# Two residual blocks in one launch: squares summed on GpSimd, compression products on 60 columns, hgrn heads in a loop

## The reference, cut to what matters

```
def rms_norm_2(u, g):                      # the memory's norm (g_mem) and the feed-forward's (g_ffn)
    y = uf * lax.rsqrt(jnp.mean(uf * uf, axis=-1, keepdims=True) + EPS)
    return (y * g).astype(u.dtype)

def compress(u, pe, w1, w2):               # once for keys, once for values; 15 windows of 32 positions, 2 heads
    blk = u[:, tok] + pe[None, None, :, None, :]
    blk = blk.transpose(0, 1, 3, 2, 4).reshape(B, n_cmp, HKV, -1)
    return (jax.nn.silu(blk @ w1) @ w2).transpose(0, 2, 1, 3)

h = rms_norm(x, hgrn_norm[j]); y = hgrn2_mixer(h, ...)   # 16 heads, two directions each
hm = rms_norm_2(mem, g_mem)
hf = rms_norm_2(x, g_ffn); gg, uu = jnp.split(hf @ w_gu, 2, axis=-1)
```

## Time and profile before

| | |
|---|---|
| median of 3 executions | 2378.72 us (2376.79 to 2382.08) |
| profiled execution | 2377.85 us, span 2376.1 us |
| TensorE (PE) busy | 2316.5 us, 97% |
| VectorE (DVE) busy | 1661.3 us, 70% |
| ScalarE (ACT) busy | 1274.4 us, 54% |
| GpSimd (POOL) busy | 226.7 us, 10%, all in the first 330 us |
| mean traffic to and from HBM | 172 GB/s |
| mean granted clock of TensorE | 0.994 |

### The profile page before, as it was taken

How to read it: one execution, slowest core, us unless ns; L and a number is a source line. 1 busy time by engine, 2 the same in 40 slices (tenths; PEclk the granted TensorE clock), 3 DMA queues, 4 the chain that set the end, 5 groups by cost and what they waited for, 6 DMA issues and landing times.

```text
span 2376.1 us, 37247 instructions
## 1 busy us (share of the span) xinstructions
PE 2316.5 (97%) x14226; PEld 2053.9 (86%) x14226; DVE 1661.3 (70%) x2540; ACT 1274.4 (54%) x1438; POOL 226.7 (10%) x53
## 2 busy tenths in 40 slices
PE   6999999999999999999999998989999999999999
PEld 6999988888888888888888877869888888888888
DVE  6777776778878887766766757756666566655666
ACT  6565565666666666455666656455333334333443
POOL 4777730000000000000000000000000000000000
PEclk9999999999999999999999999999999999999999
DMA  6444445444444443565444323524555555555556
GB/s 223 167 176 178 177 170 184 165 160 169 156 164 163 160 160 131 206 229 214 160 151 152 139 90 107 193 107 160 183 188 188 184 194 179 192 181 191 185 195 221
DMA packets 57428, 409.43 MB, mean 172 GB/s; under 512 B 6496, under 2 KB 6624, under 8 KB 8544
## 3 DMA queue, kind: packets, MB, share of 16 engines
q1 hardware_dynamic: 57312, 407.82, 48.1%
HBM read 405.70 MB, written 2.10 MB: 172 GB/s over the span
## 4 chain that ended last, share of the span: by engine, by line
PE 91%; DVE 3%; ACT 3%; issue 1%; DMA 1%; SPq 0%; ACTq 0%; DVEq 0%
PE G L350 24%; PE G L349 23%; PE G L348 12%; PE G L351 12%; PE G L357 4%; PE G L358 4%; PE G L359 4%; DMA RAW<-stream_dram 1%; ACT HI L326 1%; PE A L1010 1%; PE A L1037 1%; PE A L998 1%; DVE LO L333 0%; PE A L1012 0%; PE A L357 0%
## 5 line engine op out<-in xcount | busy, mean ns | idle before, releaser
L326 ACT ACTIVATE HI<-RAW 128x2048 fp32r<-128x2048 f32 x381 | 728.4, 1913 | 793.3 <-DMA RAW<-stream_dram 792.1
L333 DVE TENSOR_TENSOR LO<-RAW,HI 128x2048 fp32r<-128x2048 f32 x332 | 760.1, 2290 | 156.9 <-ACT HI L326 153.5
L350 PE MATMUL G<-HX,HI 128*128 128x512 f32 x1544 | 624.0, 404 | 3.3 <-DVE HX L492 2.7
L349 PE MATMUL G<-HX,HI 128*128 128x512 f32 x1544 | 612.3, 397 | 0.0
L348 PE MATMUL G<-HX,LO 128*128 128x256 f32 x1544 | 431.5, 279 | 0.0
L351 PE MATMUL G<-HX,LO 128*128 128x256 f32 x1544 | 429.8, 278 | 0.0
L350 PE MATMUL G<-HXB,HI 128*128 128x512 f32 x992 | 392.5, 396 | 2.1 <-DVE X L668 1.7
L349 PE MATMUL G<-HXB,HI 128*128 128x512 f32 x992 | 390.6, 394 | 0.0
L348 PEld LDWEIGHTS G<-HX,LO 128*128 128x128 f32 x1544 | 291.0, 188 | 70.5
L351 PEld LDWEIGHTS G<-HX,LO 128*128 128x128 f32 x1544 | 291.6, 189 | 63.5
L350 PEld LDWEIGHTS G<-HX,HI 128*128 128x128 f32 x1544 | 294.4, 191 | 8.2 <-issue 3.2
(11 more groups left out here) (357 smaller groups left out, 2652.4 us busy)
## 6 DMA issues: line engine op xcount, KB each, us to landing
RAW<-stream_dram SPq DMA_DIRECT2D x381, 1024.0 KB, 4.8
X<-x_dram SPq DMA_DIRECT2D x4, 512.0 KB, 5.4
MB<-mem_dram SPq DMA_DIRECT2D x4, 512.0 KB, 7.2
out_dram<-X SPq DMA_DIRECT2D x4, 512.0 KB, 7.7
CON<-constants_dram SPq DMA_DIRECT2D x1, 981.0 KB, 16.3
VEC<-vectors_dram SPq DMA_DIRECT2D x1, 623.5 KB, 17.3
VEC<-vectors_dram SPq DMA_DIRECT2D x1, 272.0 KB, 6.8
CON<-constants_dram SPq DMA_DIRECT2D x1, 64.5 KB, 1.9
```

Of the source, the lines that this page charges most:

```text
L326: nc.scalar.activation(HI[:, c.slot(RING), :], RAW[:, c.slot(RING), :], ACT.Copy).then_inc(hi_ready, 1)
L333: nc.vector.tensor_tensor(LO[:, c.slot(RING), :], RAW[:, c.slot(RING), :], HI[:, c.slot(RING), :].bitcast(F32), ALU.subtract).then_inc(lo_ ...
L349: return nc.tensor.matmul(res, wh, both[:, k, :, :], start=False, stop=last)
L350: nc.tensor.matmul(res, wh, both[:, k, :, :], start=first, stop=False)
```

## The change

Three things are changed.

1. GpSimd gets two programs behind its convolution part. `mem_pool` squares the memory by `tensor_tensor` of 128 x 1024 (four times), adds the groups (three times), and folds the four tiles to one (two smaller additions); TensorE then does one product with ones, after chunk ks1, in place of 16. `cross_pool` adds ScalarE's squares of the first three groups of x and folds them; TensorE does 1 + 4 products, all within the first feed-forward chunk, in place of 16.
2. BLH and BLL lie beside each other in one tile BL of 60 columns per position; a position takes two products (BL with the high and with the low part of the weights) and gives a 60 x 256 result. ScalarE copies it (no silu), the transposes become products with a "fold" matrix that adds the two halves, and silu is applied on HS.
3. The hgrn heads 4 to 15 run in a loop of three rounds with four heads each, on TensorE, ScalarE and VectorE.

```diff
-        BLH = at("BLH", [P, 2, CMP_LEN, 2 * N_CMP], F32R)
-        BLL = at("BLL", [P, 2, CMP_LEN, 2 * N_CMP], F32R)
+        BL = at("BL", [P, 2, CMP_LEN, 4 * N_CMP], F32R)
+        BLH, BLL = BL[:, :, :, 0:2 * N_CMP], BL[:, :, :, 2 * N_CMP:]
...
-                        res, l = A[2 * kv][0:2 * N_CMP, 0:2 * P], 8 * part + pos
-                        nc.tensor.matmul(res, BLH[:, kv, l, :], HI[:, c.slot(RING), w], start=(l == 0), stop=False)
-                        nc.tensor.matmul(res, BLL[:, kv, l, :], HI[:, c.slot(RING), w], start=False, stop=False)
-                        mm = nc.tensor.matmul(res, BLH[:, kv, l, :], LO[:, c.slot(RING), w], start=False, stop=(l == CMP_LEN - 1))
+                        res, l = A[2 * kv][0:4 * N_CMP, 0:2 * P], 8 * part + pos
+                        nc.tensor.matmul(res, BL[:, kv, l, :], HI[:, c.slot(RING), w], start=(l == 0), stop=False)
+                        mm = nc.tensor.matmul(res, BL[:, kv, l, :], LO[:, c.slot(RING), w], start=False, stop=(l == CMP_LEN - 1))
...
-                if name in sums_after:
-
-                    g = sums_after.index(name)
-                    pe.wait_ge(n_sq, norm_mem.sq(GRP * (g + 1)))
-                    for k in range(GRP):
-                        nc.tensor.matmul(A[5][:, 0:T], ONES, HN[:, g % 2, k, :], start=(g == 0 and k == 0),
-                                         stop=(g * GRP + k == KT - 1)).then_inc(n_ss, 1)
+                if name == MEM_SUM_AFTER:
+                    pe.wait_ge(n_sq, norm_mem.sq(KT))
+                    nc.tensor.matmul(A[5][:, 0:T], ONES, HN[:, 0, 0, :], start=True, stop=True).then_inc(n_ss, KT)
...
-                        tr = nc.tensor.transpose(A[2 * kv + 1][:, 32 * m:32 * m + 2 * N_CMP], HT[0:2 * N_CMP, kv, m * P:(m + 1) * P],
-                                                 IDENT[0:2 * N_CMP, 0:2 * N_CMP])
+                        tr = nc.tensor.matmul(A[2 * kv + 1][:, 32 * m:32 * m + 2 * N_CMP], HT[0:4 * N_CMP, kv, m * P:(m + 1) * P],
+                                              con("fold")[0:4 * N_CMP], start=True, stop=True)
...
-                    nc.scalar.activation(HT[0:2 * N_CMP, kv, :], A[2 * kv][0:2 * N_CMP, 0:2 * P], ACT.Silu).then_inc(mx_ht, 1)
+                    nc.scalar.activation(HT[0:4 * N_CMP, kv, :], A[2 * kv][0:4 * N_CMP, 0:2 * P], ACT.Copy).then_inc(mx_ht, 1)
...
-                    nc.scalar.activation(HN[:, g % 2], MB[:, g * GRP:(g + 1) * GRP, :], ACT.Square).then_inc(n_sq, GRP)
...
-                                         ACT.Copy).then_inc(mx_hs, 1)
+                                         ACT.Silu).then_inc(mx_hs, 1)
...
+        def mem_pool(pool):
+
+            sums, more = HN[:, 0], HN[:, 1]
+
+            def squares(g, out):
+                mem = MB[:, g * GRP:(g + 1) * GRP, :]
+                nc.gpsimd.tensor_tensor(out, mem, mem, ALU.mult).then_inc(pool_sum, 1)
+
+            pool.wait_ge(s_mem, 64)
+            squares(0, sums)
+            for g in range(1, KT // GRP):
+                pool.wait_ge(pool_sum, 2 * g - 1)
+                squares(g, more)
+                pool.wait_ge(pool_sum, 2 * g)
+                nc.gpsimd.tensor_tensor(sums, sums, more, ALU.add).then_inc(pool_sum, 1)
+            pool.wait_ge(pool_sum, 7)
+            nc.gpsimd.tensor_tensor(HN[:, 0, 0:2], HN[:, 0, 0:2], HN[:, 0, 2:4], ALU.add).then_inc(pool_sum, 1)
+            pool.wait_ge(pool_sum, 8)
+            pool.wait_ge(n_ss, norm_mem.sq(0))
+            nc.gpsimd.tensor_tensor(HN[:, 0, 0], HN[:, 0, 0], HN[:, 0, 1], ALU.add).then_inc(n_sq, KT)
...
-            for j in range(HEADS):
+            for j in range(4):
                 head(At(j), At(j - 1) if j else None)
+            with pe.Fori(1, 4) as i:
+                for j in range(4):
+                    head(At(j, 4, i), At(j - 1, 4, i))
...
-            def sums_x(g):
-
-                pe.wait_ge(n_sq, norm_ff.sq(GRP * (g + 1)))
+            def sums_x(pe):
+
+                res = A[norm_ff.bank][:, 0:T]
+                pe.wait_ge(pool_sum, 12)
+                nc.tensor.matmul(res, ONES, HN[:, 0, 0, :], start=True, stop=False)
+                pe.wait_ge(n_sq, norm_ff.sq(KT))
                 for k in range(GRP):
...
+                    mm = nc.tensor.matmul(res, ONES, HN[:, 1, k, :], start=False, stop=(k == GRP - 1))
+                mm.then_inc(n_ss, KT)
...
-                if cc:
-                    sums_x(cc - 1)
-            parts[0].plan = [(0, 0, 12), lambda pe: sums_x(3), (1, 0, 8), (0, 12, 16), (1, 8, 16)]
+            parts[0].plan = [(0, 0, 12), sums_x, (1, 0, 8), (0, 12, 16), (1, 8, 16)]
...
-                wait(act, n_ss, norm_ff.sq(GRP * (cc - 1)) if cc > 1 else 0)
-                nc.scalar.activation(HN[:, cc % 2], X[:, GRP * cc:GRP * (cc + 1), :], ACT.Square).then_inc(n_sq, GRP)
+                wait(act, pool_sum, 7 + cc if cc > 1 else 0)
+                nc.scalar.activation(HN[:, min(cc, 1)], X[:, GRP * cc:GRP * (cc + 1), :], ACT.Square).then_inc(n_sq, GRP)
...
+        def cross_pool(pool):
+
+            for g in (1, 2):
+                pool.wait_ge(n_sq, norm_ff.sq(GRP * (g + 1)))
+                pool.wait_ge(pool_sum, 7 + g)
+                nc.gpsimd.tensor_tensor(HN[:, 0], HN[:, 0], HN[:, 1], ALU.add).then_inc(pool_sum, 1)
+            pool.wait_ge(pool_sum, 10)
+            nc.gpsimd.tensor_tensor(HN[:, 0, 0:2], HN[:, 0, 0:2], HN[:, 0, 2:4], ALU.add).then_inc(pool_sum, 1)
+            pool.wait_ge(pool_sum, 11)
+            nc.gpsimd.tensor_tensor(HN[:, 0, 0], HN[:, 0, 0], HN[:, 0, 1], ALU.add).then_inc(pool_sum, 1)
```

More of the change, by code:

```diff
@@ L115 @@
 K_NAMES = [("ones", 128), ("eps", 1), ("ident", 128), ("keep", 2 * T), ("tri", 4 * P), ("dist1", 2 * T),
-           ("dist0", T), ("distc", 2 * 16), ("slope", 8), ("rowok", 1), ("lnsc", 1)]
+           ("dist0", T), ("distc", 2 * 16), ("slope", 8), ("rowok", 1), ("lnsc", 1), ("fold", 2 * N_CMP)]
 K_AT, n_ = {}, 0
@@ L155, in make_constants @@
     put("lnsc", np.full((P, 1), math.log(ATT_SCALE)))
+    put("fold", np.tile(np.eye(2 * N_CMP), (P // (2 * N_CMP) + 1, 1))[0:P])
     return c
@@ L439, in gres @@
             return G[:, r.slot(NG), 0:T]
-        n_zero, n_hx, scaled = sem("n_zero"), sem("n_hx"), sem("scaled")
+        n_zero, n_hx, scaled, pool_sum = sem("n_zero"), sem("n_hx"), sem("scaled"), sem("pool_sum")
         n_sq, n_ss, n_ln, n_rr, n_hn, n_hh = (sem(f"n_{s}") for s in ("sq", "ss", "ln", "rr", "hn", "hh"))
@@ L961, in build @@
         hg_zg = sem("hg_zg")
+        STEPS_ST = 15
         def order(d, s):
@@ L1128, in hgrn_act @@
             act.wait_ge(hg_oml, 2)
-            for j in range(HEADS):
+            for j in range(4):
                 head(At(j), At(j - 1) if j else None, At(j - 2) if j > 1 else None)
+            with act.Fori(1, 4) as i:
+                for j in range(4):
+                    head(At(j, 4, i), At(j - 1, 4, i), At(j - 2, 4, i))
             last = At(HEADS - 1)
@@ L1267, in hgrn_dve @@
             st = Steps(dve, hg_stp)
-            for j in range(HEADS):
+            for j in range(4):
                 head(At(j), At(j - 1) if j else None, At(j - 2) if j > 1 else None, st)
+            with dve.Fori(1, 4) as i:
+                st2 = Steps(dve, hg_stp, 4 * STEPS_ST, i, st.n - 4 * STEPS_ST)
+                for j in range(4):
+                    head(At(j, 4, i), At(j - 1, 4, i), At(j - 2, 4, i), st2)
+                st2.end()
             last = At(HEADS - 1)
@@ L1276, in hgrn_dve @@
             gate(last)
-            states(last, st)
+            states(last, Steps(dve, hg_stp, base=st.n + 3 * 4 * STEPS_ST))
             low(last - 1)
@@ L1366, in mixa_scaled @@
             return At(SCALED_MIX + results.index(name))
-        squares_after, sums_after = ["vc1", "K0", "ks0", "K1"], ["K0", "ks0", "K1", "ks1"]
+        MEM_SUM_AFTER = "ks1"
         def mixa_pe(pe):
@@ L1814, in build @@
         (gl_gk, gl_t, gl_soft, gl_la, gl_sc, gl_db, gl_exp, gl_ek, gl_qt, gl_tr, gl_s, gl_kx, gl_vt, gl_sm, gl_kv, gl_step,
-         gl_st, gl_o, gl_sq, gl_ss, gl_lr, gl_rr, gl_og, gl_y, gl_r, mk_sq, mk_ss, mk_ln, mk_rr, mk_ck, mk_tr, mk_cv, gl_zero) = (
+         gl_st, gl_o, gl_sq, gl_ss, gl_lr, gl_rr, gl_og, gl_y, gl_r, mk_sq, mk_ss, mk_ln, mk_rr, mk_ck, mk_tr, gl_zero) = (
             sem(s) for s in ("gl_gk gl_t gl_soft gl_la gl_sc gl_db gl_exp gl_ek gl_qt gl_tr gl_s gl_kx gl_vt gl_sm gl_kv gl_step "
-                             "gl_st gl_o gl_sq gl_ss gl_lr gl_rr gl_og gl_y gl_r mk_sq mk_ss mk_ln mk_rr mk_ck mk_tr mk_cv gl_zero").split())
+                             "gl_st gl_o gl_sq gl_ss gl_lr gl_rr gl_og gl_y gl_r mk_sq mk_ss mk_ln mk_rr mk_ck mk_tr gl_zero").split())
         norm_cross = Norm("g_cross", H_CROSS, C_CQ - 1, 5)
@@ L2103, in memory_dve @@
             for b in range(2):
-                nc.vector.tensor_copy(CVT[:, 2 * b:2 * b + 2, :, :].rearrange("p a t m -> p (a t m)"), A[2 + b][:]).then_inc(mk_cv, 1)
```

(11 more changed lines are left out.)

## The result

The kernel after takes 2383.17 us in the median of 20 runs (2377.09 to 2386.67), the kernel before 2378.32 in 20 runs beside it: ratio 1.0019, 95% interval 1.0013 to 1.0025. That is +4.9 us, against a forecast of +1.4, and at the edge of what the prediction calls no change; the range held it. In the profiled executions the span grew from 2376.1 to 2381.5.

A forecast was written before the change was run, and what follows sets the result against it. TensorE, working 97% of the span, was taken as the bound. Mixa +2.0, clock +2.6, cross attention -3.2 and loops 0 gave +1.4 on 2377.85, so 2379.3, stated as 2380 us; own range 2375 to 2386, whole range 2365 to 2388.

The forecast's parts named there:

- Products removed: TensorE: compression -7.2, memory's norm -6.5, feed-forward's norm -4.8, fold products +0.6; sum -17.9 us, -13.1 of it in mixa.
- Rival D: Compression: 60 columns load slower than a 256-column product runs; bounded at 0.4 us in all, no chance of its own.
- GpSimd beside VectorE: Mixa: one at a time on SBUF inputs; K1's low part +8.5, the sum after ks1 1.2 late; mixa taken at +2.0.
- rival A: GpSimd and VectorE do not disturb each other: 2366 to 2367 us; chance 0.29.
- rival B: GpSimd wins every tie: mixa +4.5, K0 late, three gaps, two clock drops, cross -2.5: 2387.5 us; chance 0.18.
- Clock: Mixa: after TensorE idles 3 us before ks0 and 7 before K1, one drop to 0.50: +2.6 (0 to 6.8).
- Table load: Mixa, between fold and second layer: silu's 1.28 us load on ScalarE no longer hidden; TensorE idles 0.9 us.
- Mixa as a whole: Mixa stage: +2.0 us with GpSimd and VectorE taking turns, plus 2.6 for the granted clock.
- Cross attention: Feed-forward norm: -4.8 of products, part lost to GpSimd's additions ahead of low parts or splits; net -3.2 us.
- chunk 3 of C_CO ends 5.2 us sooner: Sign in the cross attention's output projection: that chunk ends 5.2 us sooner after its first.
- Loops: Hgrn heads 4 to 15: loop branches and register work priced at 0.
- Rival C: Hgrn: loop bodies are refetched at branches back, +3.8 us on top of the forecast, 2384 us; chance 0.06.

The follow-up runs named there:

- the constant alone: Kernel before plus only the 30 unused columns of the fold constant, put behind the other constants: 2378.18 us, ratio 0.9996 (0.9987 to 1.0006).

## Why the prediction came out nearly right, step by step

The mechanism that carries the forecast, GpSimd and VectorE taking turns, was right. That the sum came near is in part luck. In the profiles the forecast's +1.4 became +5.4: mixa came 2.3 below its term, the cross attention's projection and what follows it 4.2 above (6.2 against kernels that hold the constant), the stages between them 2.6 and the ones ahead -0.5, which the forecast had at nothing.

**Products removed.** Right. Compression alone measured -5.2; the step's terms give -7.2 + 0.6, less the table load. Rival D's price of a wider load does not show: the 16 products of K3 take 1.87 us in the kernel after, 0.117 each.

**GpSimd beside VectorE.** The mechanism was right and decided the case: one record of 0.79 in place of 0.42 was enough to see it, and rival A, at 0.29, is ruled out by the memory's norm alone. The Trainium skill (SBUF — State Buffer, "SBUF: two separate sides") states the exclusive lock for a VectorE instruction with two SBUF inputs and a GpSimd one that reads SBUF; the trace agrees for tensor_tensor (3.12 in place of 1.00), and GpSimd's memsets, which read nothing, hold nothing up. With one GpSimd input the trace shows VectorE kept out for the first 0.9 us and not for the whole instruction; here the measurement decides.

The end of the path was right too: K1 forecast near 1069, measured 1069.59. Its division was not. I let VectorE reach K0 on time and put all 8.5 us on K1 (gaps of 3 and 7). But VectorE's path is already full ahead of K0: a scaling and four window steps meet GpSimd before the split of 1052.27, which itself took 4.10. So K0 waited 6.27, ks0 0.77, K1 3.14. That is the beginning of rival B's sequence at the forecast's price, since after 1058.4 GpSimd was done and the rest ran free. That K1 came within 0.3 us is partly luck. The forecast had both engines at work without a break until 1067.0 and the two small additions behind that; in the trace the small additions (3.21 and 0.74) were among what VectorE met, and from 1058.4 on it spent 3.2 us on waits for ScalarE and a reduction, beside which GpSimd had nothing left to do.

**Clock.** Forecast +2.6 for one drop; there were two, 6.8 us from 1052.5 and 3.4 from 1069.6. More than half of the first was spent in the wait. What was lost stands in the chunks: K0's 16 products took 3.2 and K1's 3.4, where K3's took 1.87, so 2.9 in all. The size was right by a different road.

**Table load.** Forecast 0.9. In the kernel after 0.30, since a 0.57 wait for a low part ahead of kw0 moved the fold back; in compression alone 1.72, where V2's high part stood ahead of the load. The step lacked ScalarE's queue.

**Mixa as a whole.** Forecast +2.0 and the clock's 2.6, so +4.6. From hgrn's end (948.73 before, 948.26 after) to the first transposes behind mixa (1140.24 and 1142.10) the stage grew by 2.3. The waits (11.1 us in all) and the 2.9 at half clock against -13.1 of products give +0.9; the rest is pace without a wait, of which the constant alone shows 0.5 (192.03 against 191.51).

**Cross attention.** This is the step that failed: forecast -3.2. The part alone gives +1.7 (interval -0.5 to +3.8), and in the kernel after the stage from the start of the output projection to the last product is 2.95 us longer than in nine kernels that hold the constant and leave this stage alone (773.43 against 770.48). So the term was mis-sized by 5 to 6 us. It read, "the low parts of the third group come about 1.0 late for k-tiles 8 to 11". TensorE waited 5.8 for them (5.5 in the part alone), from the last product of C_CO on.

Three things were wrong. First, TensorE does not take k-tiles 0 to 7 while 8 to 11 are missing: the plan's first entry, (0, 0, 12), has one wait ahead of all twelve. Eight k-tiles are some 2.8 us at full clock; how the 1.0 was worked out does not stand in the prediction, so whether it counted on them stays open. Second, the 0.5 of spare time a chunk (5.76 - 5.25) was not there: in its second chunk VectorE waits 1.22 for ScalarE's high part of the feed-forward's first chunk, and from the split of 1617.91 on its chain runs without a hole until the third group is done, so that its 5.7 of standing reach TensorE whole. Third, the small GpSimd additions also fell in the path: line 2320 shows 5.22, which is 3.5 of standing, where the large addition, over at 1629.55, accounts for 2.3.

The sign "chunk 3 of C_CO ends 5.2 us sooner" did not come either: its last product starts 22.83 us after the stage's first, not 26.42, so 3.6 sooner, since only two groups of sums stood ahead of it. A new drop of the clock follows, in the kernel after at 1629:

```profile
1629.50:1636.20 6.70, 3.56 (x12) 3.11 (x13) 5.13 (x9) 2.43 (x5) 2.15 (x3) 0.50 0.25 103
```

The stage's own terms close: 5.8 of waits, -4.8 of products, and some 1.8 for the 3.5 us after the wait at half clock, +2.8 of the 2.95.

**Loops.** Right for the time: 0. Rival C is ruled out by the loops alone. The Trainium skill (Runtime: NRT & Kernel Launch, "Instruction fetch mechanics") would let VectorE stall at its branches, and the trace agrees. In the kernel after VectorE stands twice, four heads apart, at the two branches back, for nothing that the profile names; the loops alone show the same (3.73 and 3.67), kernels without these loops have no such stop in hgrn:

```profile
671.21 2.29 DVE L334 TENSOR_TENSOR LO<-RAW,HI 128x2048 fp32r<-128x2048 f32 x1 [3.69 <-issue]
802.62 2.29 DVE L334 TENSOR_TENSOR LO<-RAW,HI 128x2048 fp32r<-128x2048 f32 x1 [3.80 <-issue]
```

That is twice the 1.9 of the earlier trace rows. TensorE does not wait for it, and 0.9997 says that it costs nothing here: VectorE waits for others in this place anyway (0.79 for ScalarE in the kernel before) and catches up within the head.

**What is left.** The single parts add up to +1.0 us by their ratios (-5.2, -0.7, +5.2, +1.7), the whole has +4.5. But each of these four kernels holds the constant, and the constant alone has -1.0 us (-3.1 to +1.4), so the sum has it four times and the whole once. Counted once, the parts give +4.0. Each single ratio is uncertain by some 2 us, so as far as these runs can tell the parts add. One more thing shows in the profiles: the feed-forward norm alone has nearly the wait of the kernel after (5.49 against 5.83), but its stage is only 1.03 longer and not 2.95, because the loop behind it runs denser there. Windows of the kernel after, then of the feed-forward norm alone:

```profile
1640.00:1840.00 200.00, 200.00 (x1134) 173.94 (x1134) 129.59 (x138) 80.43 (x71) 0.00 (x0) 1.00 0.51 184
```
```profile
1640.00:1840.00 200.00, 200.00 (x1145) 174.54 (x1144) 130.62 (x140) 82.39 (x72) 0.00 (x0) 1.00 0.53 185
```

Both are busy without a break at full clock, with the same code; the kernels with nothing changed there have 1134 to 1137. So the part alone was flattered in its profile. And 2.6 us of the profiled +5.4 lie where the change does nothing: from mixa's end to the output projection the kernel after takes 461.60 us, the two profiles of before 459.02 and 458.57, the loops alone 461.71, memory and compression together 458.39. The stretch of low clock behind 1359 lasted 10.2 us in the first and the fourth of these and 6.8 in the others, so it goes with no part of the change; what sets its length is open.

## What to carry to other kernels

Work given to an idle GpSimd is free only where it does not meet VectorE's operations with two SBUF inputs: here its two-input operations kept VectorE out for nearly their whole length, one-input ones for their first 0.9 us, and memsets not at all. Count the work of both engines as one queue, and do so up to every part that the bound engine needs, not only up to the last: here K0 came first. Read the code for what each wait covers before giving a late part a cover. Short products at the joints of a sequence, such as the sums here, may be the cover of the next part: before removing them, subtract them from the slack, not only from the sum. And split a change with several parts early: here one part gained 5 us, and another gave it back alone. Where each part carries a side effect of its own, such as a new constant, measure that alone too, or it is counted once for every part.

## What the runs showed that was not expected

- Beside GpSimd's memsets VectorE keeps all its durations (1.00, 0.66, 2.29); beside its tensor_scalar the window addition keeps 1.00, the subtraction is held for up to 0.8, and the tensor_scalar itself is stretched from 2.78 to 4.17.
- A loop body of four hgrn heads makes VectorE stand 3.7 to 3.8 us at each branch back, and TensorE does not notice.
- 30 unused columns of a constant shift the pace of products that wait for nothing: +1.6 us over 14 heads of hgrn, and -1.98 us (770.48 against 772.46, the same in both profiles of before and within 0.01 in nine kernels with the constant) from the output projection's start to the last product. In the window 1840 to 2040 the kernel before has 1139 recorded products, the constant alone 1145.

  TensorE is never idle in either, and the clock is 1.00. What sets the pace is open; no run here tells data placement from code placement. It means that a stage can differ by 1 to 2 us between two kernels without any work in it having changed, and that parts of this size add up only roughly.
